# Dealing the query work of a routing period over its sixteen batches, turning the slots first, and spreading the batches over the list operations

## The reference

```python
def peer_retrieve(h, wq, keys):
    q = (h @ wq).reshape(N, PEER_HEADS, 2, PEER_DHALF)
    s = jnp.einsum('nhpc,hpkc->nhpk', q, keys)          # 16 lists of 128 scores a token
    sv, si = lax.top_k(s, PEER_TOPK)                    # best 16 of each list
    comb = sv[:, :, 0, :, None] + sv[:, :, 1, None, :]
    cv, ci = lax.top_k(comb.reshape(N, PEER_HEADS, 256), PEER_TOPK)
    expert = i1 * PEER_NKEYS + i2                       # i1, i2: si taken at ci // 16, ci % 16
    gate = jax.nn.softmax(cv, axis=-1)
```

## Time and profile before

| | |
|---|---|
| median of three runs | 3333.01 us |
| profiled execution | 3337.24 us |
| its span | 3335.6 us |
| busy: PE, DVE, ACT, POOL | 3045.6, 2407.0, 935.2, 1489.0 us |
| routing with a placement (five periods) | 712.87 to 1138.30 us of the span |

### The profile page before, as it was taken

The page is one execution under the profiler, slowest core; times in us unless marked ns, Lnnn a source line. Parts: engine busy times, 40 slices in busy tenths (PEclk is TensorE's granted clock), DMA queues, the critical chain, the costliest instruction groups (busy, mean ns, idle before and its releaser), DMA issues.

```text
span 3335.6 us, 43974 instructions
## 1 busy us (share of the span) xinstructions
PE 3045.6 (91%) x16658; PEld 2331.2 (70%) x16658; DVE 2407.0 (72%) x4987; ACT 935.2 (28%) x1271; POOL 1489.0 (45%) x1188
## 2 busy tenths in 40 slices
PE   8899978577888469999999999999999999999997
PEld 1466644245555369988888887888888888788886
DVE  1233324999988878887777777878777777778798
ACT  0111111138888622222222222222122222212222
POOL 0010000425554334346656565656565565666453
PEclk9999989889999879999999999999999999999999
DMA  9711131602222367789999999999999999999883
GB/s 357 212 64 63 57 145 64 208 7 108 108 108 108 151 223 264 265 292 353 366 351 366 359 350 368 353 370 353 355 351 369 349 360 344 352 347 336 307 295 140
DMA packets 305919, 858.73 MB, mean 257 GB/s; under 512 B 25376, under 2 KB 108832, under 8 KB 303984
## 3 DMA queue, kind: packets, MB, share of 16 engines
q0 software_dynamic: 151344, 551.09, 45.1%
q1 hardware_dynamic: 154333, 305.79, 25.6%
q10 hardware_dynamic: 108, 0.22, 0.0%
HBM read 793.86 MB, written 63.15 MB: 257 GB/s over the span
## 4 chain that ended last, share of the span: by engine, by line
PE 50%; DMA 5%; POOL 4%; DVE 3%; issue 2%; ACT 0%; DVEq 0%; SPq 0%; ACTq 0%
PE y_ps L1889 22%; PE a_ps L1870 20%; PE picked_ps L1907 5%; DMA shared<-in_peer_u,ids 3%; PE uT_ps L1857 3%; POOL shared L1453 2%; POOL quad L1464 1%; DMA shared<-in_peer_v,ids 1%; DVE uT_lo L1615 1%; DVE shared L1674 1%; DVE shared L1644 0%; DMA quad<-in_peer_v,idsT 0%; DVE shared L1657 0%; ACT uT_hi L1534 0%; DVE m_lo L1630 0%
## 5 line engine op out<-in xcount | busy, mean ns | idle before, releaser
L1453 POOL DMA_INDIRECT shared<-in_peer_u,ids x480 | 560.7, 1168 | 595.3 <-DVE acts L1657 507.1
L1657 DVE CUSTOM_DVE_ANT_0 shared<-shared 128x1024 f32<-128x1024 f32 x480 | 579.2, 1221 | 173.5 <-DMA shared<-in_peer_u,ids 172.9
L1870 PE MATMUL a_ps<-h_hi,uT_lo 128*128 128x320 f32 x2048 | 643.8, 314 | 1.7 <-DVE h_lo L1786 1.7
L1870 PE MATMUL a_ps<-h_hi,uT_hi 128*128 128x320 f32 x2048 | 633.8, 309 | 0.0
L1870 PE MATMUL a_ps<-h_lo,uT_hi 128*128 128x320 f32 x2048 | 633.8, 309 | 0.0
L1889 PE MATMUL y_ps<-v_hi,m_lo 128*128 128x512 f32 x1280 | 511.5, 400 | 25.7 <-DVE shared L1644 14.6
L1644 DVE TENSOR_TENSOR shared<-shared,y_ps 128x512 f32<-128x512 f32 x630 | 422.5, 685 | 150.2 <-PE y_ps L1889 149.5
L1889 PE MATMUL y_ps<-v_lo,m_hi 128*128 128x512 f32 x1280 | 504.6, 394 | 0.0
L1889 PE MATMUL y_ps<-v_hi,m_hi 128*128 128x512 f32 x1280 | 502.3, 392 | 0.0
L1464 POOL DMA_INDIRECT quad<-in_peer_v,idsT x384 | 443.9, 1156 | 120.1 <-issue 120.1
L1870 PEld LDWEIGHTS a_ps<-h_hi,uT_lo 128*128 128x128 f32 x2048 | 386.1, 189 | 7.2 <-issue 2.1
(11 more groups left out here) (187 smaller groups left out, 4197.2 us busy)
## 6 DMA issues: line engine op xcount, KB each, us to landing
shared<-in_peer_u SPq DMA_DIRECT2D x128, 512.0 KB, 7.5
v_all<-in_peer_v SPq DMA_DIRECT2D x128, 512.0 KB, 7.5
gate_blocks<-dense SPq DMA_DIRECT2D x10, 4096.0 KB, 12.1
gates<-gate_blocks SPq DMA_DIRECT2D x64, 640.0 KB, 22.1
w_ada<-in_w_ada SPq DMA_DIRECT2D x12, 2048.0 KB, 11.7
x_in<-in_x_prompt SPq DMA_DIRECT2D x16, 512.0 KB, 4.5
shared<-in_peer_u,ids POOLq DMA_INDIRECT x480, 8.7
shared<-in_w_in SPq DMA_DIRECT2D x8, 768.0 KB, 13.2
```

The source lines that it names most:

```text
L1453: pool.indirect_dma_start(out=rows[n % 4], out_offset=None, in_=u_table if n < DOTS else v_table, in_offset=bass.IndirectOffsetOnAxis(ap=i ...
L1657: nc.vector.tensor_tensor_reduce(out=rows[n % 4], in0=rows[n % 4], in1=token_row, scale=1.0, scalar=0.0, op0=ALU.mult, op1=ALU.add, accum_ ...
L1870: last = nc.tensor.matmul(a_ps[n][:, 0:GROUP], lhs[s][:, k, :], rhs[:, k, tok], start=k == 0 and m == 0, stop=k == KD - 1 and m == 2)
```

## The change

The same instructions run in another order within a period. On PE `turn_slots` comes first; then each batch from 0 to 11 is followed by three, three or two steps of a query block, so that a block ends with batches 2, 5, 8 and 11; the transposes stand two batches later, the scores at batches 9, 10, 12 and 15. On ACT the copy of a block stands at the batch with which it ends, that of the transpose three batches later; the first `widen_keys` is at batch 11, exp and the second at batch 15. On DVE batch 0 stands behind the first sixteen MAX8, one batch behind every three searched lists, and the short rank operations have none left between them.

```diff
+        QUERY_ENDS, SCORED = (2, 5, 8, 11), (9, 10, 12, 15)
 # ACT, period
-                if prepare is not None:
-                    take_q(prepare, 0)
                 if indexed is not None:
                     take_index(indexed)
                 if placed is not None:
                     take_slots(placed)
-                if prepare is not None:
-                    take_qT(prepare, 0)
-                    take_q(prepare, 1)
                 for b in range(BATCHES):
                     if placed is not None:
                         left_rows(placed - FIRST_DENSE, b)
                         if b:
                             take_gates(placed - FIRST_DENSE, b - 1)
-                    if prepare is not None and b in (4, 8):
-                        take_q(prepare, b // 4 + 1)
-                    if prepare is not None and b in (1, 5, 9):
-                        take_qT(prepare, b // 4 + 1)
-                    if choose is not None and b == 6:
+                    if prepare is not None and b in QUERY_ENDS:
+                        take_q(prepare, QUERY_ENDS.index(b))
+                    if prepare is not None and b - 3 in QUERY_ENDS:
+                        take_qT(prepare, QUERY_ENDS.index(b - 3))
+                    if choose is not None and b == 11:
                         widen_keys(choose, 0)
-                    if choose is not None and b == 12:
+                    if choose is not None and b == 15:
                         act.wait_ge(S.shifted, choose + 1)
                         nc.scalar.activation(soft[:, :, :], soft[:, :, :], ACT.Exp).then_inc(S.exp, 1)
-                    if choose is not None and b == 14:
                         widen_keys(choose, 1)
 # DVE, two_lists: rows(0) ahead of the searches, rows(1) to (5) after every third list
+                rows(0)
                 own.settle()
 ...
-                rows(0)
+                    if n % 3 == 2:
+                        rows(1 + n // 3)
 ...
-                rows(10)
+                rows(15)
 # PE, period
-                if prepare is not None:
-                    product(prepare, 0)
                 if done is not None:
                     turn_slots(done)
-                if prepare is not None:
-                    product(prepare, 1, range(0, 5))
-                    if done is not None:
-                        pe.wait_ge(S.slotsT, done * 2 + 2)
-                    turn(prepare, 0)
-                    product(prepare, 1, range(5, KD))
                 for b in range(BATCHES):
                     if placed is not None:
                         place(placed - FIRST_DENSE, b)
-                    if prepare is not None:
-                        if b < 8:
-                            product(prepare, 2 + b // 4, range(b % 4 * 2, b % 4 * 2 + 2))
-                        if b in (0, 4, 8):
-                            turn(prepare, b // 4 + 1)
-                        if b in range(9, 13):
-                            scores(prepare, b - 9)
+                    if prepare is None:
+                        continue
+                    if b - 2 in QUERY_ENDS:
+                        if b - 2 == QUERY_ENDS[0] and done is not None:
+                            pe.wait_ge(S.slotsT, done * 2 + 2)
+                        turn(prepare, QUERY_ENDS.index(b - 2))
+                    if b <= QUERY_ENDS[-1]:
+                        product(prepare, b // 3, range(b % 3 * 3, min(b % 3 * 3 + 3, KD)))
+                    if b in SCORED:
+                        scores(prepare, SCORED.index(b))
```

More of the change, by code:

```diff
@@ L984, in two_lists @@
                     own.mark(nc.vector.max(best[:, n, high], work3[:, n, :]))
-                rows(1)
+                    if n == 7:
+                        rows(6)
                 own.settle()
@@ L989, in two_lists @@
                     own.mark(nc.vector.max_index(best_at[:, n, high], best[:, n, high], work3[:, n, :]))
-                rows(2)
+                    if n in (3, 9, 15):
+                        rows(7 + n // 6)
                 own.settle()
@@ L993, in two_lists @@
                 nc.vector.tensor_copy(best_key[:, :, :], best_at[:, :, :]).then_inc(S.best_key, 1)
-                rows(3)
             def best_pairs(t, rows):
@@ L1007, in best_pairs @@
                         ALU.add))
-                rows(4)
                 own.settle()
@@ L1013, in best_pairs @@
                         own.mark(nc.vector.max(pair[:, h, part], sums[:, h]))
-                    rows(5 + n * 3)
+                    rows(10 if part is low else 13)
                     own.settle()
@@ L1018, in best_pairs @@
                         own.mark(nc.vector.max_index(pair_at[:, h, part], pair[:, h, part], sums[:, h]))
-                    rows(6 + n * 3)
+                    rows(11 if part is low else 14)
                     own.settle()
@@ L1024, in best_pairs @@
                             own.mark(nc.vector.match_replace(sums[:, h], pair[:, h, low], sums[:, h], NEG))
-                        rows(7)
+                        rows(12)
                         own.settle()
@@ L1038, in chosen_ranks @@
                 own.mark(nc.vector.tensor_scalar(narrow[:, :, :], pair_at[:, :, :], NW, None, ALU.is_ge))
-                rows(10)
+                rows(15)
                 own.settle()
                 own.mark(nc.vector.tensor_tensor(ranks[:, :], digits[:, 2:4], digits[:, 0:2], ALU.subtract))
-                rows(11)
                 own.settle()
@@ L1046, in chosen_ranks @@
                     .to_broadcast([P, 2, HEADS, TOPK]), ALU.mult))
-                rows(12)
                 own.settle()
                 own.mark(nc.vector.tensor_tensor(ranks[:, :], ranks[:, :], digits[:, 0:2], ALU.add))
-                rows(13)
                 own.settle()
@@ L1055, in chosen_ranks @@
                 own.mark(nc.vector.tensor_copy(rank[:, 1], ranks[:, 1]))
-                rows(14)
                 own.settle()
@@ L1067, in chosen_ranks @@
                     .then_inc(S.first_keyed, 1)
-                rows(15)
                 dve.wait_ge(S.key_wide, t * 2 + 2)
```

## The result

The changed kernel took 3453.93 us (median of 4 runs, 3451.03 to 3460.48) against 3337.18 for the kernel before on the same chip: a ratio of 1.0354, 95% interval 1.0325 to 1.0383. It is slower, and the forecast of 3438 with its range of 3385 to 3480 holds it. The profiled span grew from 3335.6 to 3453.7 us, by 118.1.

What follows compares the result with a forecast made beforehand. DVE's work list was taken to fill the period, ACT close behind. Copy waits and slow starts add 98.5 us in five placed periods, other periods 6: 3337.2 + 104.5 = 3441.7, less 4.2 for the median, 3438 us (3385 to 3480).

Steps and rivals of the forecast that it cites:

- The sum of 104.5 us: Whole kernel: predicted added time, 98.5 us in the five placed periods plus 6 us in the other periods.
- The slow starts: PE places after 3.7 us gaps run partly at 1.2 GHz: 1.7 us lost each, 25 us in all.
- the chain: Placed periods: ACT and PE alternate at query copies; three batches take 17.1 us, 18.8 with the slow start.
- the first rival: No slow starts: same copy waits but PE's clock stays up, 25 us less, 3412 us; chance 0.22.
- The gap: PE idle from the end of query steps to the next place: 0.5 + 3.2 = 3.7 us.
- The tail: End of placed period: second widened keys at 98.0 us behind gates and exp, then 1.95 and 4.9, ending at 104.8.
- The other periods: Periods without a dense place: first 1.5 us, second about 2.3 and 2.0, third nothing; about 6, bounds 2 and 12.
- The spreading on DVE: Batches spread among DVE's lists earn nothing, since DVE waits for `left` from batch 5 or so on.
- the early slots: Turning slots first on PE starts `left` at about 4.2 instead of 16.4 us: up to 12 us a period gained.
- The rival of free tables: DVE's tables lose most of 18.3 us a period, ACT sets the pace: period 76.4, total 3296 us; chance 0.07.
- PE end to end: Copies hidden, PE's 32 query steps behind batch 0 set the pace: 15 us less, 3318 us; chance 0.06.
- Half clock throughout: Gaps keep PE at 1.2 GHz in the whole placement: about 44 us more a period, 3660 us; chance 0.07.

Runs made afterwards that it cites:

- copy_later: Changed kernel with only ACT's query-block copies one batch later (3, 6, 9, 12 instead of 2, 5, 8, 11): 3328.9 us, ratio 0.9975 to the kernel before.
- copy_same_batch: Kernel before with ACT's copies of the third and fourth query block one batch earlier, in the batch where the block ends: 3373.8 us, ratio 1.0109.
- spread_only: Kernel before with the change's DVE order and the matching ACT places of widened keys and exp; slots and query work as before: 3327.9 us, ratio 0.9975.
- lists_as_before: Changed kernel with the DVE order of the kernel before; PE and ACT as changed: 3499.1 us, ratio 1.0490 to the kernel before.
- wider_spread: first_block_ahead2 with batches dealt out after every fourth DVE list operation, exp and second widened keys at batch 14: 3298.2 us, ratio 0.9889 to the kernel before.
- first_block_ahead2: Changed kernel, first query block whole before batch 0, then two steps a batch, copies at batches 1, 4, 8, 12, unplaced periods' first widened keys at 6: 3314.4 us.
- gaps_filled: Changed kernel with twelve added constant products on PE behind the query blocks ending with batches 5, 8 and 11: 3435.1 us, ratio 1.0291 to the kernel before.

## Why the prediction was right

The mechanism is the one forecast, shown by copy_later and copy_same_batch from both sides. The sum of 104.5 us is 13.6 short of the 118.1 by which the span grew: 6.4 in the placed periods, 4.6 in the others, 2.6 behind them. By its steps, in us from the period's start:

| step | predicted | measured |
|---|---|---|
| `left` of batch 0 | 4.2 | 3.9 |
| of batches 3, 6, 9, 12 | 22.0, 40.8, 59.6, 82.5 | 22.4, 41.0, 60.6, 82.5 |
| ACT's wait for each copy | some 5 | 5.00, 5.43, 5.43, 6.32 |
| PE's gap | 3.7 | 3.62, 4.09, 4.09, then 5.89 |
| loss of the place after it | 1.7 | 1.70, 1.80, 1.42, 1.80 |
| batch 15, second widened keys, end | 94.1, 98.0, 104.8 | 94.4, 99.0, 105.9 |

*The slow starts* were given 25 us in all, for three gaps a period; the fourth, ahead of batch 12, was rightly left out of the chain, since ACT then waits only 0.30 us. All four gaps behind a copy were followed by a slow place, and filling two of them returned 3.2 to 3.3 us a period where the place of batch 12 stayed slow, against 3.4 by the forecast: right in mechanism and size, and the first rival (none) is out. The size had some luck. The prediction took 1.7 us because "both longer gaps lost it", but the one of 3.47 us in the earlier trace rows, the nearest to the 3.7 forecast, lost 0.68 (2.63 against 1.95); by that row the sum would have been 15 us less.

*The gap* was worked out as the copy plus a batch. From the second chain on, the copy of the transposed block stands in it too, 0.47 us (870.36 to 870.83): the 0.4 us by which 4.09 exceeds the forecast. Ahead of batch 12 the widened keys add 1.80 (910.52 to 912.32).

*The tail.* The prediction had the second widened keys follow ACT's gates and exp. They were held by DVE's first product of keys instead (0.56 us idle), 1.0 us later than forecast. From there the forecast's 1.95 and 4.9 us held.

*The other periods* were given 6 us and cost about 10.6. The first (some 2 against 1.5) and the second (4.7 against 4.3) came out; the second's goes with the order on DVE (82.2 us in spread_only, 77.3 in lists_as_before and in the kernel before). The third was costed at nothing and cost 3.5: the step compared the end of PE's and ACT's work (some 36 us into the period; the fourth copy came at 36.8) with the 42 us of DVE's lists, but the first widened keys now stand behind that copy, and DVE needs them at 36.1. ACT first, then DVE, in the third period:

```profile
712.30 0.60 ACT L872 ACTIVATE q<-q_ps 128x512 f32<-128x512 f32 x1 [8.96 <-PE q_ps L1155]
712.79 0.59 ACT L877 ACTIVATE qT<-x_ps 128x512 f32<-128x512 f32 x1
713.27 1.91 ACT L902 ACTIVATE key_wide<-best_key 128x2048 bf16<-128x2048 bf16 x1
```
```profile
715.28 1.22 DVE L1060 TENSOR_TENSOR work<-work,key_wide 128x2048 bf16<-128x2048 bf16 x1 [3.68 <-ACT key_wide L902]
```

DVE waited 3.68 us for keys that had stood far ahead of its need. It is the same fault as the main one: an operation was moved behind one that waits. Of the 118.1 us, 104.9 and 10.6 are told by this; 2.6 lie behind the five periods and stay unexplained.

*The spreading on DVE* was said to earn nothing here, and that nearly held. DVE's whole order, taken back, costs 45 us (lists_as_before), but 8.7 of the 10.5 us a placed period are the later batch 0, which the prediction counted with the early slots. At most the other 1.8 us or so are the spreading's, since the chain through ACT and PE sets the pace. Alone on the kernel before, which hasn't this chain, the order earns 3.0 us a placed period.

*The rival of free tables* was right to be given little. With the copies out of the way (copy_later) the period was 81.7 us, not 76.4, and the tables still took 34.6 us of it (116.3 and 56.5 in five). The Trainium skill ("SBUF — State Buffer", section "SBUF: two separate sides") says that an operation of DVE in a fast mode and one of GpSimd shut each other out whole, and so do one of DVE with two inputs in SBUF and one of GpSimd that reads SBUF. The tables are of the second kind. The rows of wider_spread agree (last section). They show what the rival missed: spreading the tables does not end the loss, it passes much of it to other operations that then stand beside GpSimd's product, those in fp32 too (L1042 2.50 us in wider_spread, 0.42 in first_block_ahead2 as L1043). The 76.4 us that the rival named were reached in wider_spread (382.6 / 5), but by emptying DVE's idle time: 36.3 of the 42.6 us gained on the kernel before, against 6.3 of busy time.

*PE end to end* (3318) supposed the copies hidden and is near to what the version with late copies gives (3328.9), but by another limit: in copy_later's five periods DVE was busy 384.4 of 408.3 us and PE 330.5. *Half clock throughout* is out: places in a row took 1.95 us and the granted clock over the five periods was 0.84.

## What to carry to other kernels

On an engine that runs in the written order, a copy out of PSUM belongs at least one step behind the one whose matmuls it waits for, if the next input of the same matmul engine is queued behind it; a whole batch of slack cost nothing here, and its absence 125 us. When moving one such wait, look at everything that is queued behind it, in the periods without a placement too. And before pricing a loss as recoverable by spreading, compare the engine's total busy time in a trial: it tells a loss that goes from one that moves.

## What the runs showed of the hardware

- Idle time alone does not tell whether TensorE's clock falls. The place of batch 15 kept its speed after 2.19 us of idleness in the changed kernel (first row), and took 3.35 us after 2.18 us in gaps_filled (second; the granted clock of its first 2 us was 0.61). A place in copy_same_batch kept its speed after 3.65 us (third; 1.00), where the changed kernel's after 3.62 took 3.65. What else decides was not separated.

```profile
927.45 2.02 PE L1193 MATMUL place_ps<-left,right 128*128 128x128 f32 x16 [2.19 <-ACT dense L920]
```
```profile
921.01 3.35 PE L1193 MATMUL place_ps<-left,right 128*128 128x128 f32 x16 [2.18 <-ACT dense L920]
```
```profile
753.20 2.02 PE L1200 MATMUL place_ps<-left,right 128*128 128x128 f32 x16 [3.65 <-ACT dense L918]
```

- The exclusion between DVE and GpSimd is symmetric in these rows: in wider_spread the product of keys beside GpSimd took 3.28 us instead of 1.22, and the product of GpSimd that started during a comparison of 2.28 us on DVE took 4.29 instead of 2.4. DVE, then GpSimd, in order of time:

```profile
859.99 2.28 DVE L1055 TENSOR_TENSOR work<-rank,iota_rank 128x4096 bf16<-128x4096 bf16 x1
862.31 3.28 DVE L1062 TENSOR_TENSOR work<-work,key_wide 128x2048 bf16<-128x2048 bf16 x1
```
```profile
860.22 4.29 POOL L848 TENSOR_TENSOR right<-right_hot,gateT 128x1024 f32<-128x1024 bf16 x1 [2.55 <-DVE right_hot L1112]
866.94 2.37 POOL L848 TENSOR_TENSOR right<-right_hot,gateT 128x1024 f32<-128x1024 bf16 x1 [2.43 <-DVE right_hot L1112]
```
